# Hybrid decoder layer on Trainium2: 14 in-projection tiles move from the attention turns to a stage of seven pairs by seven block products

## What is computed

```python
h = rms_norm(x, g_pre_mix)
cb, cc, ch, q, k, v, ga, gb = jnp.split(h @ w_in, IN_SPLITS, axis=-1)   # 6 x 512 + 2 x 1024 columns
conv_u, conv_state = causal_dwconv(cc * ch, conv_prev, w_conv_a)        # 3 taps, per channel
y_a = (cb * conv_u) @ w_a
o = stick_breaking(q, k_all, v_all, sb_bias)                            # 8 heads of 64
y_b = o @ w_b
merged = jax.nn.sigmoid(ga) * y_a + jax.nn.sigmoid(gb) * y_b
x = x + rms_norm(merged @ w_o, g_post_mix)
```

## Time and profile before

| | us |
|---|---|
| median of the runs | 1672.57 |
| profiled execution, first to last instruction (its span) | 1670.3 |
| before the first turn's v tile | 46.0 |
| a turn's q, k and v tiles (second turn, 173.2 to 213.3) | 40.1 |
| its 28 slots (213.3 to 325.7) | 112.4 |
| end of the fourth turn | 630.2 |
| 21 pairs of the up-projection (853.6 to 1303.7) | 450.1 |

### The profile page before, as it was taken

The page is one execution under the profiler, slowest core; times in us unless marked ns, Lnnn a source line. Parts: engine busy times, 40 slices in busy tenths (PEclk is TensorE's granted clock), DMA queues, the critical chain, the costliest instruction groups (busy, mean ns, idle before and its releaser), DMA issues.

```text
span 1670.3 us, 27043 instructions
## 1 busy us (share of the span) xinstructions
PE 1659.3 (99%) x9033; PEld 1456.2 (87%) x9033; DVE 1104.3 (66%) x1619; ACT 798.6 (48%) x1399; POOL 299.2 (18%) x255
## 2 busy tenths in 40 slices
PE   9999999999999999999999999999999999999998
PEld 8999999999999999988878888888888888888886
DVE  7364255335633646548688888888888698776576
ACT  7445344444534453226554444444444454465675
POOL 2000000000000000001046666666664000000000
PEclk9999999999999999999999999999999999999999
DMA  5312221232123114453232222222222861345333
GB/s 190 91 59 70 87 72 54 65 92 68 62 67 95 49 62 150 150 171 108 77 98 80 79 79 79 79 77 71 76 79 92 287 227 59 96 146 189 114 123 117
DMA packets 176598, 170.64 MB, mean 102 GB/s; under 512 B 16207, under 2 KB 144555, under 8 KB 176492
## 3 DMA queue, kind: packets, MB, share of 16 engines
q1 hardware_dynamic: 165546, 164.41, 30.5%
q10 hardware_dynamic: 10946, 4.91, 1.0%
HBM read 129.66 MB, written 39.62 MB: 101 GB/s over the span
## 4 chain that ended last, share of the span: by engine, by line
PE 97%; DVE 2%; issue 0%; ACT 0%; POOL 0%; DMA 0%; SPq 0%; DVEq 0%; POOLq 0%; ACTq 0%
PE pair L3209 11%; PE pair L2856 9%; PE pair L2858 9%; PE pair L2857 9%; PE pair L3269 8%; PE pair L3271 8%; PE pair L3270 8%; PE pair L2810 5%; PE pair L3407 4%; PE pair L3409 4%; PE pair L3408 4%; PE pair L3278 2%; PE pair L3078 2%; PE pair L2787 2%; PE pair L2786 2%; PE pair L2785 2%
## 5 line engine op out<-in xcount | busy, mean ns | idle before, releaser
L2856 PE MATMUL pair<-xh,wh 128*128 128x384 f32 (+1 forms) x936 | 318.9, 341 | 0.0
L2858 PE MATMUL pair<-xh,wl 128*128 128x384 f32 (+1 forms) x936 | 306.2, 327 | 0.0
L2857 PE MATMUL pair<-xl,wh 128*128 128x384 f32 (+1 forms) x936 | 305.7, 327 | 0.0
L2856 PEld LDWEIGHTS pair<-xh,wh 128*128 128x128 f32 x936 | 176.4, 188 | 5.5 <-issue 4.0
L2857 PEld LDWEIGHTS pair<-xl,wh 128*128 128x128 f32 x936 | 176.5, 189 | 0.0
L2858 PEld LDWEIGHTS pair<-xh,wl 128*128 128x128 f32 x936 | 175.8, 188 | 0.0
L1090 POOL TENSOR_TENSOR hn<-hn 128x512 f32<-128x512 f32 x4 | 5.2, 1288 | 810.7 <-DVE hn L2339 810.7
L3407 PE MATMUL pair<-woph,foph 128*128 128x512 f32 x308 | 120.6, 392 | 0.0
L3409 PE MATMUL pair<-woph,fopl 128*128 128x512 f32 x308 | 120.1, 390 | 0.0
L3408 PE MATMUL pair<-wopl,foph 128*128 128x512 f32 x308 | 120.1, 390 | 0.0
L1411 ACT ACTIVATE keep<-pair,bias 128x512 f32<-128x512 f32 (+4 forms) x100 | 58.3, 583 | 115.5 <-DVE pair L2177 71.5
(11 more groups left out here) (444 smaller groups left out, 4285.8 us busy)
## 6 DMA issues: line engine op xcount, KB each, us to landing
rawp<-in_w_up SPq DMA_DIRECT2D x88, 256.0 KB, 3.8
raw<-in_w_in SPq DMA_DIRECT2D x80, 256.0 KB, 3.2
wd<-in_w_down SPq DMA_DIRECT2D x55, 256.0 KB, 3.1
f_spill<-cv SPq DMA_DIRECT2D x22, 552.0 KB, 2.8
f<-f_spill SPq DMA_DIRECT2D x44, 256.0 KB, 5.3
gat<-gate_spill SPq DMA_DIRECT2D x16, 544.0 KB, 4.5
x_spill<-x SPq DMA_DIRECT2D x16, 512.0 KB, 3.1
gate_spill<-stg SPq DMA_DIRECT2D x32, 192.0 KB, 1.9
```

The source lines that it names most:

```text
L2856: t_.matmul(b, h, xhi, start=(k == 0), stop=False, skip_group_check=True)
L2857: t_.matmul(b, h, xlo, start=False, stop=False, skip_group_check=True)
L2858: ins = t_.matmul(b, l, xhi, start=False, stop=(k == KD - 1), skip_group_check=True)
```

## The change

- The opening now makes C and H of conv tile 0 in place of q and k (`first` jobs).
- A new stage of seven pairs follows it: `WIDE_PAIRS` takes two gate tiles, or C and H of one conv tile, or two B tiles at a time. Each pair is seven block products (`wide_product`) and the samples' product. Its x sums (`wsum`, four of 2048 columns a partition with high and low part) are made once by DVE and ACT in front of and in the first pair, whose order is `1S267543`. POOL makes each pair's weight sums and multiplies the factors of the conv. DVE runs the taps in one block (`convolve`). Results go to `gate_spill` and `c_spill`.
- The four turns have six tiles each: q, k, v and three gate tiles as filling, so 72 pieces over the same 28 slots. All turns use the score form of the later turns, and `new_rows(vT, 0)` comes behind slot 0's pieces. The loops over the turns on ACT, DVE and SyncE are unrolled.

```diff
+FIRST_JOBS = 2
+FILL_JOBS = 3
+NIN = 3 + FILL_JOBS
+IN_JOBS = FIRST_JOBS + NC4 * NIN
+IN_FILL = NG * FILL_JOBS
+def first_piece(n):
+    return n * IN_FILL * KD // SLOTS
...
+WIDE_PAIRS = [("g", 0), ("c", 1), ("b", 0), ("c", 2), ("c", 3), ("b", 2), ("g", 1)]
+def wide_order(n):
+    return "1S267543" if n == 0 else "162S7543"
...
@@ SyncE
+            hold(p_x0, 4)
+            wide_load(0)
+            for n in range(NW):
+                if n + 1 < NW:
+                    hold(d_wl, W_LOW["h1" if n else "c", n])
+                    wide_load(n + 1)
...
@@ GpSimd
+            def wide_sums(n):
+                pool.wait_ge(w_in_, 64 * (n + 1))
+                if n:
+                    pool.wait_ge(d_wl, W_LOW["c", n - 1])
+                else:
+                    pool.wait_ge(p_x0, 2 * NBK)
+                minus(wtc[:, 0, :, :], w[:, 1, 0:KH, :], w[:, 0, 0:KH, :]).then_inc(g_wt, 1)
...
+            wide_sums(0)
+            for n in range(NW):
+                if n + 1 < NW:
+                    wide_sums(n + 1)
+                if WIDE_PAIRS[n][0] != "g":
+                    wide_times(n)
...
@@ ScalarE
+            def wide_c11(n):
+                act.wait_ge(p_wq, wide_done(n, "2"))
+                if kind == "c":
+                    act.wait_ge(d_c, len([k for k in CONV_AFTER if k < n]))
...
+                if n == 0:
+                    sum_high(2, 3)
+                wide_sc(n)
+                if n == 0:
+                    sum_high(3, 4)
+                wide_c11(n)
+                if n + 1 < NW:
+                    wide_h(n + 1, 0)
+                    wide_b(n + 1)
...
@@ VectorE
+            conv_by(0)
+            x0_scaled(7, 2, 6, 0)
+            x0_low(6)
+            x0_low(7)
+            x0_low(8)
+            v.memset(uc[:, 0:2], 0.0)
...
+            then(raw_sum(0, block_of(xh, 0, 1), block_of(xh, KH, 1), ALU.add, ALU.add, block_of(xl, 0, 1)))
+            v.tensor_tensor(wsraw[0][:, :, :], wsraw[0][:, :, :], block_of(xl, KH, 1), ALU.add).then_inc(d_ws, 1)
+            conv_by(1)
+            dve.wait_ge(d_ws, 1)
+            raw_sum(1, wsraw[0][:, :, :], block_of(xh, 0, 0), ALU.subtract, ALU.subtract, block_of(xl, 0, 0)).then_inc(d_ws, 1)
+            wide_h(0, 0)
+            wide_h(0, 1)
+            sum_low(1)
+            wide_b(0)
+            conv_by(2)
+            sum_low(0)
+            wide_c(0)
+            dve.wait_ge(d_ws, 2)
+            raw_sum(2, block_of(xh, KH, 1), wsraw[1][:, :, :], ALU.subtract, ALU.add, block_of(xl, KH, 1)).then_inc(d_ws, 1)
+            sum_low(2)
+            then(v.tensor_tensor(wsraw[3][:, :, :], block_of(xh, KH, 0), wsraw[1][:, :, :], ALU.subtract))
+            v.tensor_tensor(wsraw[3][:, :, :], wsraw[3][:, :, :], block_of(xl, KH, 0), ALU.add).then_inc(d_ws, 1)
...
+            for n in range(NW):
+                if n:
+                    c12(n - 1)
+                    wide_h(n, 1)
+...
+                if n == 0:
+                    sum_low(3)
+                summed(n, "u3", "7", wu3[:, :], wu2[:, :])
+                if n > 1 and n - 1 in CONV_AFTER:
+                    dve.wait_ge(g_wm, W_TIMES[n - 1])
+                    convolve(CONV_AFTER[n - 1])
+                if n + 1 < NW:
+                    wide_h(n + 1, 0)
+                wide_free(n)
+                summed(n, "c22", "5", wide0[1][:, HALF:SEQ], wu3[:, :])
...
@@ TensorE, wide_pair(n)
+                    if what == "1":
+                        pe.wait_ge(d_wl, W_LOW["h0", n])
+                    elif what == "7":
+                        if n: pe.wait_ge(d_wq, W_SUM["c21", n - 1])
+                        else: pe.wait_ge(d_wl, W_LOW["S3",])
+                    elif what == "4":
+                        pe.wait_ge(d_wq, W_SUM["u3", n])
+                    elif what == "3":
+                        pe.wait_ge(d_wq, W_SUM["c22", n])
+                        if n == 0: pe.wait_ge(d_wl, W_LOW["S4",])
...
@@ TensorE, slots
-                    for i in range(PIECES):
-                        piece(*divmod(PIECES * n + i, KD))
-                        if n == 0 and i == 2:
-                            new_rows(vT, 0)
+                    for i in range(first_piece(n), first_piece(n + 1)):
+                        piece(*divmod(i, KD))
+                    if n == 0:
+                        new_rows(vT, 0)
```

More of the change, by code:

```diff
@@ L743, in gate_out, with ended, pair @@
                                  stg[g][:, 0:w]).then_inc(stg_out[g], 16)
-            gtn = Count()
-            def pair(c, last):
+            def ended(c, next0, next1):
+                load(next0)
+                for n in range(FILL_JOBS - 2):
+                    gate_out(c, n)
+                load(next1)
+                for n in range(FILL_JOBS - 2, FILL_JOBS):
+                    gate_out(c, n)
+            def pair(c):
                 load(in_job(c, 2))
-                hold(p_m, miscn.at(2))
+                hold(p_m, miscn.at(1))
@@ L1268, in _, with conv_in @@
             vno, soo, att = Count(), Count(), Count()
-            def pair(c, first, last=False):
+            def conv_in(gr):
+                act.wait_ge(p_unit, 2 * gr + 1)
+                b = banks[0][:, 0:GROUPS[gr][1]]
+                for d, cols in padded(uc, gr):
+                    ins = s_.activation(d, like(b[:, cols], d), ACT.Copy)
+                ins.then_inc(a_u, 1)
+            x0_high(3)
+            conv_in(0)
+            x0_high(4)
+            x0_square(7)
+            x0_high(5)
@@ L2054, in backwards, with conv_by @@
                 return bass.AP(x.tensor, x.offset + x.shape[1] - 1, [x.ap[0], (-1, x.shape[1])])
-            def pair(c, first, last=False):
+            def conv_by(gr):
+                dve.wait_ge(p_unit, ENDS[0] + 1 if gr == NG - 1 else 2 * gr + 2)
+                dve.wait_ge(a_u, gr + 1)
+                b = banks[1][:, 0:GROUPS[gr][1]]
+                for d, cols in padded(uc, gr):
+                    ins = v.tensor_tensor(d, like(b[:, cols], d), d, ALU.mult)
+                ins.then_inc(d_u, 1)
@@ L2058, in unit_in, with pair @@
+            wlo()
+            c12(NW - 1)
+            unit.step(PAIR1)
+            dve.wait_ge(p_wq, 8 * NW)
+            dve.wait_ge(d_wq, len(W_SUM))
+            for h in range(2):
+                v.memset(f(kl[h])[other(h), :], 0.0)
+            def pair(c, last=False):
                 def unit_in(j, gr):
-                    u = unit_of(j, gr, first)
-                    dve.wait_ge(p_unit, unit.at(u + 1))
+                    u = 3 * (FIRST_JOBS + NIN * c + j) + gr
+                    dve.wait_ge(p_unit, u + 1)
@@ L2170, in pair @@
+                wlo()
+                for gr in range(NG):
+                    q_low(gr)
+                wlo()
+                for gr in range(NG):
+                    k_low(gr)
+                wlo()
+                qbn.step(2)
                 for n in range(SLOTS):
@@ L2195, in pair @@
                     i = FILL_AT.get(n)
[L2196 to L2202 removed]
+                    if i is not None and i % 3 == 0:
+                        wlo()
                     if last and n == NSTEP + 1:
@@ L2869, in idle, with in_tile, opening @@
+            def in_tile(j, gr, between={}):
+                b = open_unit(j, gr)
+                for k in range(KD):
+                    for what, n in between.get(k, ()):
+                        what(n)
+                    step(b, j, gr, k)
+            def opening():
                 def idle(i):
@@ L2935, in block_low_last @@
                     ins.then_inc(p_unit, 1)
+                idle(1)
+                pe.wait_ge(d_ones, 1)
+                pe.wait_ge(row_in, 16)
+                for i in range(2):
+                    ins = t_.matmul(banks[i], ones[:, :], grow[:, 512 * i:512 * i + 512], start=True, stop=True)
+                ins.then_inc(p_mix, 1)
+                idle(0)
+                x0_turn(0)
+                x0_turn(1)
+                by_blocks()
+                weight_low_last(1, 0, {1: 3, 7: 4, KD + 1: 5})
```

902 lines of the change are left out of this document (523 added, 379 removed).

## The result

The changed kernel takes 1743.1 us (median of 4 runs, 1741.0 to 1746.3), the kernel before 1672.4 in the same session: ratio 1.0425, 95% interval 1.041 to 1.044. The profiled execution has a span of 1740.4 us, 70.1 more than the 1670.3 of before. The forecast was 1723, with +50 for the span. The direction held, and so did the range (1688 to 1746), 3 us from its upper end; the size was 20 us short.

A forecast was written before the change was run, and what follows sets the result against it. PE, holding 97% of the chain, was taken as the bound. Terms -17.8 (PE's work), +23 (opening, pair 0), +10 (pairs 1 to 6), +35 (slots) made +50; 1670.3 + 50 + 2.3 = 1723 us, range 1688 to 1746.

The forecast's parts named there:

- PE's own work, -17.8: Opening, seven pairs and four turns: PE's timeline alone, no wait counted, ends at 612.4 instead of 630.2, 17.8 us less.
- Opening and pair 0, +23: Opening's end and first pair: PE waits 17 us for DVE's x sums, plus 6 for POOL; between 6 and 28.
- The 2.3 at product 1: Pair 0: PE stalls 2.3 us before product 1, behind two more sums and the first low part on DVE.
- POOL's 6 us: Opening's end and pair 0: POOL's eight weight sums slow DVE by about 7 us, 6 of it on the path.
- The estimate of 10 us: Pair 0: by the skill's port rule POOL's eight sums cost DVE 10 us in place of 6, 4 us more.
- Pairs 1 to 6, +10: New stage: product 3 waits for c22 behind DVE's conv block, most in pair 4; 10 us, between 3 and 16.
- Slots, +35: Four turns: with 72 pieces PE waits for ACT's and DVE's chains, 8.8 us a turn; between 16 and 52.
- The clock, a rival: Gaps of 3 to 7 us in the first pair lower PE's clock: 8 us more, 1731; above 1746 has 0.06.
- Queues, "at nothing": SyncE's loads and spills in pairs and turns: costed at nothing; a late load would be 2 to 4 us once.
- Signs: Expected profile: beta/scan waits 30 to 40 us in total, slots 70 to 76 us, pairs 1 to 6 21 to 26 each.
- Rival "the slots absorb it": Turns: the look-ahead of two slots suffices, 3 us a turn in place of 8.8, time 1700; chance 0.16.
- Rival "faster": New stage and slots: all waits together stay under 17.8 us, net -6, time 1667; chance 0.08.

The follow-up runs named there:

- the last version: Changed kernel with plain first pair, uneven filling, SyncE's order altered, conv taps between u2 and u3, three more order edits: 1675.3 us, ratio 1.0024.

## Why the prediction was right, and where it was short

- **PE's own work, -17.8: right.** Undisturbed pairs of the changed kernel take 21.4 to 21.8 us (forecast 21.2), and 21.2 in the last version; what is behind the turns did not change.
- **Opening and pair 0, +23: right in sum, in part by luck.** Pair 1 started at 88.0 for 88.4. The waits at product 7 (7.3), in the opening (4.4) and at product 4 (3.0) stand where they were put (7.2, 3.0, 4.0). The 2.3 at product 1 did not come, since the opening's last unit ran at 1.2 GHz and ended later. DVE had product 4 ready 2.4 us earlier than laid out (80.8 for 77.2 with POOL's 6 on top), and the clock, which was not in the sum, took 1.6 back behind it. The run with the sums cut shows that DVE's sums set the end. **POOL's 6 us** were measured at 5.9 in the sums (seven of them took 2.6 to 3.4 us for 2.29) and at 5.8 in the run without POOL's reads. Both engines were stretched: POOL took 3.2 to 3.3 for 1.30. One sum and one subtraction thus take 3.3 us side by side, where one behind the other would be 3.6. The rule of the Trainium skill ("SBUF — State Buffer", section "SBUF: two separate sides"), one holds and the other waits, is near this for such a pair. The estimate of 10 us by it was too high for pair 0 all the same: two of the eight subtractions kept their 1.30 us.
- **Pairs 1 to 6, +10: two things were put at nothing.** The pairs cost 14.6. The mechanism (DVE's conv block ahead of c22, in pair 4 also ahead of ACT's copy) was right: one tap in place of three took 2.8, 4.8 and 2.7 us off pairs 2, 4 and 5. But POOL's weight sums were priced in pair 0 alone. They stretched the conv blocks as well, and without them the six pairs took 5.5 us less. Pair 4 was sized at 4.4 and measured 7.8: 2.8 of it is POOL's stretch of the block, 2.0 the clock in product 3, and the 3.0 left are less than the forecast had for the waits themselves.
- **Slots, +35: right.** 8.6 to 8.9 us a turn of idle time (7.0 as listed, with 0.17 to 0.2 more for each wait of PE, whose ends are modelled) for 8.8. With the filling restored the waits were gone. Another 2 us of the turns no run names.
- **The clock, a rival and not a term.** "No row shows it in mid-kernel" was true and was taken for a reason to leave it out. The clock fell in eight places, three of them at the start of slots after waits of 1.7 us, shorter than the gaps of 3 to 7 us to which the rival tied it. It cost 4.9 us in the turns (4.1 by the run with the taps behind c22, which had no fall there either), 2.0 in pair 4 and 1.6 in pair 0, together near the 8 that the rival named, though in other places. The warning of the Trainium skill ("TensorE: Matmul & The Clock Gate", section "Why this matters for your kernels"), of idle gaps of PE between bursts, agrees with the falls behind the long waits. It says nothing of whether they are on the path.
- **Queues, "at nothing".** The loads were looked at one by one, each "wanted 12 us later". The queue's own time was not added up: 8.1 us of page issues and 2.0 of read-back, behind a spill that ends with the stage. The price named for a late load, "2 to 4 us once", was 6.3. In pair 3 too the load for pair 4 was on the edge, as the run with the taps behind c22 brought to light.
- **Signs.** The turns' waits (28.1 us in total) are under the 30 to 40 that were named, and pair 4 is over the 21 to 26. The slots of the second turn take 75.8 us (115.9 less the 40.1 of its q, k and v part), in the 70 to 76. PE's share of the chain can't be read, as said above.
- **Rival "the slots absorb it": refuted** with the uniform split, and nearly true with another one: a turn then takes 108.4 us, 3.5 over PE's own 104.9, where the rival said 3, and no work was moved to or from an engine.
- **Rival "faster": its condition** was all waits under 17.8 us. The last version came near and missed it.

What stays open: some 2 us of the turns, and why the clock fell in some turns and not in others with the same waits.

## What to carry to other kernels

When filling leaves a chain, price each gap by the cover that stands in it, and deal out what filling is left by the chains' lengths: the same pieces in other slots were worth 27 us here. Add up a queue's own issue time across a hand-over as if it were an engine, and look for an idle stretch of the late engine before moving a block on it: one block of some 5 us made PE wait in two places and was free in a third. An engine beside the late one (POOL here) is to be priced in every stage where it runs: its cost in the pairs behind the first was nearly that of the first. A wait of PE that is removed only moves if what stands behind it in the same queue was late too.

## What the runs showed of the hardware

- The granted clock fell to 1.2 GHz for 3.4, 6.8 or 10.2 us in mid-kernel, and in turns of the same program with the same waits (1.7 us ahead of the second turn of value rows) it fell in some and not in others: in the run with the plain first pair turns of 115.5 and 115.6 us had a fall and the one of 114.0 between them had none.
- Ahead of a wait for DVE, PE at half rate cost nothing: pair 1 started at 88.0 us with the clock at 0.77 and at 0.96. Behind the last wait it cost in full: product 3 of pair 4 took 4.7 us for 2.7.
- DVE's sum of 2048 elements took 2.29 us alone, 2.64 to 3.36 beside POOL's subtractions, and 2.28 to 2.29 beside POOL's memsets of the same tiles. A DVE copy of two elements took 1.21 us beside a subtraction of POOL and 0.17 without.
- The same 1 MB load, issued at 143.33 us in the changed kernel and at 143.35 in the one with matmuls in the waits, was first read by POOL at 149.64 and 151.51.
